# Expert weights of a mixture-of-experts step read in 16 KB pieces, and tokens turned with matching strides

## The reference, cut to what matters

```
hu = jnp.einsum('td,edf->tef', xt, w_gate_up)     # d 2048, f 1024
hg, hv = jnp.split(hu, 2, axis=-1)
act = jax.nn.silu(hg) * hv * gates[..., None]     # 512 features for each expert
out = jnp.einsum('tef,efd->td', act, w_down)      # d 2048
```

## Time and profile before

| | us |
|---|---|
| median of 3 runs | 1817.91 (1817.19 to 1818.08) |
| the profiled execution | 1817.13 |
| its span, first to last instruction | 1815.1 |
| PE busy | 1659.0 (91%) |
| DVE busy | 1313.6 (72%) |
| ACT busy | 1070.6 (59%) |
| granted TensorE clock, mean | 0.953 |

### The profile page before, as it was taken

The page is one execution under the profiler, slowest core; times in us unless marked ns, Lnnn a source line. Parts: engine busy times, 40 slices in busy tenths (PEclk is TensorE's granted clock), DMA queues, the critical chain, the costliest instruction groups (busy, mean ns, idle before and its releaser), DMA issues.

```text
span 1815.1 us, 20866 instructions
## 1 busy us (share of the span) xinstructions
PE 1659.0 (91%) x7572; PEld 1200.1 (66%) x7572; DVE 1313.6 (72%) x1658; ACT 1070.6 (59%) x1223; POOL 45.0 (2%) x34
## 2 busy tenths in 40 slices
PE   6999997897799999999999958869999999999995
PEld 5777775895576666766666636556665675665664
DVE  1333334654678998998998856567899899899887
ACT  1132224333657787787787842355877777777774
POOL 0000000000000000000000000000001001000100
PEclk9999999899889999999999977888999999999998
DMA  9443436252479999999999962266998999998990
GB/s 285 141 153 113 150 127 208 93 177 101 156 280 325 388 366 329 400 357 344 378 360 341 372 220 93 98 226 249 369 368 333 339 389 332 344 385 330 337 381 14
DMA packets 146405, 487.90 MB, mean 269 GB/s; under 512 B 5324, under 2 KB 59276, under 8 KB 126892
## 3 DMA queue, kind: packets, MB, share of 16 engines
q1 hardware_dynamic: 141328, 463.75, 69.7%
q0 software_dynamic: 2464, 13.37, 2.5%
q10 hardware_dynamic: 2522, 9.59, 1.6%
HBM read 476.15 MB, written 14.47 MB: 270 GB/s over the span
## 4 chain that ended last, share of the span: by engine, by line
PE 77%; DVE 12%; issue 4%; ACT 3%; DMA 2%; ACTq 1%; DVEq 0%; POOL 0%; POOLq 0%
PE ps L997 17%; PE ps L999 16%; PE ps L998 16%; PE ps L830 14%; DVE ring_lo L1415 6%; PE ps L859 2%; PE ps L861 2%; PE ps L860 2%; PE ps L1042 2%; PE ps L841 2%; PE ps L915 1%; DVE xtok L1373 1%; DVE zstat L1377 1%; DMA xtok<-x_rows,src_now 1%; PE ps L923 1%
## 5 line engine op out<-in xcount | busy, mean ns | idle before, releaser
L1415 DVE TENSOR_TENSOR ring_lo<-ring,whi 128x1024 fp32r<-128x1024 f32 x768 | 922.1, 1221 | 115.7 <-ACT whi L703 108.3
L703 ACT ACTIVATE whi<-ring 128x1024 fp32r<-128x1024 f32 x768 | 806.2, 1060 | 256.2 <-PE ps L999 249.2
L997 PE MATMUL ps<-whi,operands 128*96 128x512 f32 x1536 | 625.0, 407 | 35.3 <-issue 17.6
L999 PE MATMUL ps<-ring_lo,operands 128*96 128x512 f32 x1536 | 610.7, 398 | 0.0
L998 PE MATMUL ps<-whi,operands 128*96 128x512 f32 x1536 | 608.9, 396 | 0.0
L997 PEld LDWEIGHTS ps<-whi,operands 128*96 128x96 f32 x1536 | 250.4, 163 | 169.4 <-DVE ring_lo L1415 40.4
L999 PEld LDWEIGHTS ps<-ring_lo,operands 128*96 128x96 f32 x1536 | 251.1, 163 | 112.4 <-issue 0.2
L998 PEld LDWEIGHTS ps<-whi,operands 128*96 128x96 f32 x1536 | 252.7, 165 | 100.1 <-issue 0.8
L830 PE MATMUL ps<-xT,ring 128*128 128x288 f32 x1024 | 249.7, 406 | 0.7 <-ACT mark L571 0.7
L830 PEld LDWEIGHTS ps<-xT,ring 128*128 128x128 f32 x1024 | 194.4, 190 | 54.6 <-ACT mark L571 0.8
L859 PE MATMUL ps<-operands,whi 128*128 128x288 f32 x256 | 76.7, 300 | 17.3 <-DVE ylo L1205 17.3
(11 more groups left out here) (263 smaller groups left out, 1039.9 us busy)
## 6 DMA issues: line engine op xcount, KB each, us to landing
ring<-in_moe_w_gate_up SPq DMA_DIRECT2D x128, 2048.0 KB, 9.1
ring<-in_moe_w_down SPq DMA_DIRECT2D x64, 2048.0 KB, 9.9
ring<-in_lru_w_in SPq DMA_DIRECT2D x16, 2048.0 KB, 9.6
ring<-in_lru_w_out SPq DMA_DIRECT2D x8, 2048.0 KB, 8.5
x_rows<-xtok ACTq DMA_DIRECT2D x4, 1024.0 KB, 3.9
ring<-in_pool_w SPq DMA_DIRECT2D x4, 1024.0 KB, 6.4
xtok<-in_x_prompt SPq DMA_DIRECT2D x2, 1024.0 KB, 9.2
ring<-in_lru_w_a SPq DMA_DIRECT2D x8, 256.0 KB, 5.4
```

The source lines that it names most:

```text
L703: eng.activation(whi[:, i % NPART, :], ring_at(n)[:, at * PART:(at + 1) * PART], ACT.Copy)\
L997: mm(o, hi, whi[:, i % NPART, cols], start=start, stop=False)
L999: last = mm(o, hi, lo_at(base + i // PARTS_CHUNK, i % PARTS_CHUNK)[:, cols], start=False, stop=stop)
L1415: TT_(lo_at(n, at), ring_at(n)[:, at * PART:(at + 1) * PART], whi[:, i % NPART, :].bitcast(F32), ALU.subtract).then_inc(lo_ready, 1)
```

## The change

The views of the weights in HBM, of the token rows and of the activations change; no instruction is added or removed.

```diff
@@ window_loads
-                        src = w[bass.ds(at, 128 * SLOT)].rearrange("(k p f) -> p k f", k=k, p=128)
+                        src = w[bass.ds(at, 128 * SLOT)].rearrange("(p k f) -> p k f", k=k, p=128)
@@ turn_rows
+                    rows = XS[:, q * 512:(q + 1) * 512].rearrange("w (p k) -> w k p", k=4)
                     for b in range(4):
-                        k = 4 * q + b
-                        last = nc.tensor.transpose(ps[:, 6 + q % 2, b * W:(b + 1) * W], XS[:, k * 128:(k + 1) * 128],
-                                                   ident[0:W, 0:W])
+                        last = nc.tensor.transpose(ps[:, 6 + q % 2, b * W:(b + 1) * W], rows[:, b, :], ident[0:W, 0:W])
@@ transpose_act
+                        rows = th[0:W, :].rearrange("w (c p k) -> w c k p", c=2, k=2)
                         for f in range(KF):
-                            last = nc.tensor.transpose(ps[:, 6 + e % 2, f * W:(f + 1) * W],
-                                                       th[0:W, f * 128:(f + 1) * 128], ident[0:W, 0:W])
+                            last = nc.tensor.transpose(ps[:, 6 + e % 2, f * W:(f + 1) * W], rows[:, f // 2, f % 2, :],
+                                                       ident[0:W, 0:W])
```

## The result

The changed kernel takes 1819.33 us (median of 20 runs, 1814.35 to 1822.23), the kernel before 1817.15 us (20 runs, 1814.25 to 1818.71). The ratio is 1.0013 with a 95% interval of 1.0007 to 1.0019: 2.2 us slower, inside the 0.2% that I had called no change. The profiled execution is 1819.58 us with a span of 1817.6, where before had 1815.1.

A forecast was written before the change was run, and what follows sets the result against it. TensorE's own list was taken as the bound, with loads never waited for. Loads 0 plus stepped transposes +1.7 us, on 1817.9 us, gave 1819.6 us, range 1815.5 to 1828.

The forecast's parts named there:

- part 1: The expert weight loads in 16 KB pieces: worth 0 us, bounds -1.8 and 0, since SP's queue waits for slots.
- Rival 2: Expert weight loads: 16 KB pieces as dear as 1 KB ones become the bound, 98 us more, 1916 us; chance 0.04.
- rival 3: Expert weight loads: DMA still cut into small pieces, packets near 146,000, time 1819.6 us; chance 0.07.
- L800's 112 ns: Spacing of L800's 20 loads with steps of 16 or 64 bytes, taken as upper bound for a stepped transpose.
- rival 1: Transposes in windows: stepped loads become PE's pace, 26 us, 1844 us, or 1831 with the 16-byte step alone; chance 0.13.
- rival 4: VectorE's L1415: fewer, longer slot writes speed its reads from 1224 to 1198 ns, -4.6 us, 1813 us; chance 0.05.

The follow-up runs named there:

- loads_only: The kernel before with only the 16 KB loads of the changed kernel, transposes left without a step: 1816.14 us against 1816.73, ratio 0.9997.
- extra_turn: The kernel before with the last transpose of each group done once more, no steps or other loads: 1818.0 us, ratio 1.0001.

## Why the prediction was right, point by point

**The bound and the loads.** That PE's list sets a window's length and that a load is never waited for held, before and after, and loads_only shows it directly: 0.9997. So part 1's value of 0 was right, and so was what pays for it, the wait of SP's queue (1149.2 us in the earlier trace rows; in after ScalarE still never waits for a DMA in its reads of the ring). Its price for 16 KB was not. I had 38.4 us for a MB and a share of 84%; the window gives 16 x 143.4 x 0.902 / 49.87 = 41.5 us and 90%, hardly under before's 42 us. The 38.4 came from a stretch of 12 us, and the trace of after gives 101.5% of 12 us for 5.16 MB there, 37.8, in the same place; in the place of the earlier trace rows it gives 92.2% of 26 us for 9.01 MB, 42.6, where before had 43.4. In both places the larger piece saved under 2%, while the places differ by 12%: the place was cheap, not the piece. The margin to the 45.6 us from which the loads would set the pace was thus 4 us in place of 7. Rival 2 stayed on its side of it, and rival 3 fell with the packets.

**The turns.** The bounds were right: 85 and 112 ns for a stepped transpose, and 106 ns came out. So L800's 112 ns did hold as an upper bound. That its stretch ran at the lower clock was taken from its durations; the windows view has 1.00 for 12 to 15 us, and no row shows the lower clock there. What the step costs at the lower clock is seen better at the 16 transposes of L923 ahead of the first window, of which a first run of eight is shown here, with the clock, for before and then for after:

```profile
476.00:479.00 3.00, 2.21 (x13) 1.92 (x14) 2.73 (x4) 1.91 (x3) 0.00 (x0) 0.50 0.00 0
476.25 1.51 PE L923 MATMUL ps<-ident,xtok 96*128 96x96 f32 x8 [7.47 <-DMA xtok<-x_rows,src_now]
```

```profile
476.40 1.53 PE L923 MATMUL ps<-ident,xtok 96*128 96x96 f32 x8 [7.56 <-DMA xtok<-x_rows,src_now]
```

Eight take 1.51 us without and 1.53 us with the step: next to nothing, as the prediction had it for these. The value inside the bounds was mis-sized. I took half of the difference for L923 and nothing for L947, 1.7 us; both cost 0.11 us a group, 7.0 us, close to the upper bound of 7.8. The failed step is that I let the size of the step decide. The page on SBUF of the Trainium skill (SBUF — State Buffer, Door 1), with lines of 16 bytes that give full rate from two hits in a line on, would also have L947 cheaper, since its step of 8 bytes leaves two columns in a line. The measurement decides: two columns in a line (8 bytes), one (16 bytes) and one in every fourth line (64 bytes) take 106, 106 and 102 ns.

**What the sum left out.** The clock. The prediction's sum had no term for it, though the earlier trace rows showed 0.99 in each window and the chain 2.44 us of standing in the earlier trace rows. With the cost of 7.0 us in the windows the clock stayed up in four of eight gaps, which gave 5.6 us back; that it did so because the gaps moved in time is argued, not shown. The forecast of +1.7 us against the measured +2.2 is luck: two errors of opposite sign nearly cancel, 5.3 us too little for the turns and 5.6 us of clock not thought of (what is left of the 2.2, beyond 7.0 - 5.6 = 1.4, lies outside the windows). Without the second the kernel would have come out 7 us slower, at 1824 to 1825 us; that is still in the range, but it is slower by over 0.2%.

**The marks.** A group of four was to stay at 0.49 to 0.50 us, up to 0.58; it is 0.60, 0.02 over the upper mark and below the 0.65 where rival 1 was to begin. The period of a window was to be 143.4 to 143.9 us; it is 144.1 to 144.3 in layer 0 where the clock falls as in before, 0.7 to 0.9 us longer, as eight groups of 0.11 us make it. The chain in order of time, to be laid beside the earlier trace rows:

```profile
537.48 2.43 issue
...
681.82 2.44 issue
...
825.93 2.44 issue
```

L1415 is unchanged at 1221 ns on average, so rival 4 fell too.

## What to carry to other kernels

A transfer that nobody waits for can't be improved into time, whatever its busy share says; look for its waiter first. A transpose that reads its operand with a step costs about 20 to 28 ns more at the higher clock, even for a step of two floats, and where TensorE's list is the bound each of them reaches the end, unless the clock gives it back. Where the engine stands for a short while in each turn of a loop, compare the clock at that place in both kernels before a difference of some microseconds is put down to the edit; and ask of each such gap which producer the wait really needs, since here one count too many was worth 1.8 to 2.0%, far more than the layout.

## What the runs showed of the hardware that I had not expected

- A load of 128 stepped fp32 columns for a transpose takes 205 to 218 ns against 141 without a step, at the higher clock, for steps of 8, 16 and 64 bytes. At the lower clock (0.50) eight transposes took 1.53 us against 1.51.
- The same gap of 2.44 us was followed by a fall of the granted clock in one window and not in another of the same execution. A fall cost 1.3 to 1.4 us (26.6 to 26.9 us for the stretch around the gap against 25.3 to 25.6, in six kernels). Added work of 5.3 us on the engine that is the bound (extra_turn) did not show in the time (1.0001, 0.9986 to 1.0015).
- Pieces of 16 KB in place of 4 and 8 KB leave a MB at 41.5 us of one engine's time against 42. The stretch of the program in which it is read (37.8 and 42.6 us in after) matters more than the piece.
